# mLSTM row sums as a 257th value column of the numerator products

## What is computed

```python
sc = jnp.einsum('bhtd,bhsd->bhts', qc, kc) * jnp.exp(D - m_t[..., None])
num = jnp.einsum('bhts,bhsd->bhtd', sc, vc) + inter[..., None] * (...)
den = sc.sum(-1) + inter * (...)
h = num / jnp.maximum(jnp.abs(den), jnp.exp(-m_t))[..., None]
```

## Time and profile before

| | us |
|---|---|
| median of 3 runs | 1370.7 |
| lowest, highest | 1369.31, 1373.73 |
| profiled execution | 1371.72 |
| its span | 1369.7 |
| mean granted clock of TensorE | 0.988 |
| TensorE, VectorE, ScalarE, GpSimd busy | 1343.4, 800.8, 639.0, 206.5 |

### The profile page before, as it was taken

One profiled execution on the slowest core, in us unless ns is written; L12 is line 12 of the kernel. 1 busy time (PEld: TensorE's weight loads), 2 busy tenths in 40 slices (PEclk: granted clock), 3 DMA queues, 4 the chain that ended last, 5 costly groups with the idle time before them and its releaser, 6 DMA issues.

```text
span 1369.7 us, 16279 instructions
## 1 busy us (share of the span) xinstructions
PE 1343.4 (98%) x6400; PEld 1108.8 (81%) x6400; DVE 800.8 (58%) x1180; ACT 639.0 (47%) x883; POOL 206.5 (15%) x248
## 2 busy tenths in 40 slices
PE   9999999999999999999799999999999999999995
PEld 8888888888788888888688888888888888888884
DVE  5655555555657664865764554555546576657656
ACT  5445445444455543443444454454444555435432
POOL 0410310311211000300311122121121200003002
PEclk9999999999999999999999999999999999999998
DMA  9864664664466566466376646646635656555562
GB/s 314 268 182 132 187 175 138 184 172 136 138 181 187 170 200 202 148 189 199 107 239 187 175 129 190 179 129 190 178 108 166 187 174 191 173 200 166 185 192 87
DMA packets 127002, 240.86 MB, mean 176 GB/s; under 512 B 12048, under 2 KB 12080, under 8 KB 126416
## 3 DMA queue, kind: packets, MB, share of 16 engines
q1 hardware_dynamic: 123936, 230.85, 56.1%
q0 software_dynamic: 1632, 6.90, 1.4%
q10 hardware_dynamic: 1360, 2.10, 0.4%
HBM read 237.72 MB, written 2.10 MB: 175 GB/s over the span
## 4 chain that ended last, share of the span: by engine, by line
PE 90%; DVE 5%; ACT 2%; DMA 2%; issue 0%; SPq 0%; DVEq 0%; ACTq 0%
PE ps L302 81%; DMA w_raw<-w_in_dram 2%; DVE w_lo L812 1%; ACT w_hi L600 1%; PE ps L403 1%; DVE xres L1133 1%; PE ps L377 1%; PE ps L535 1%; ACT arena L651 1%; DVE xres L1122 1%; PE ps L319 1%; PE ps L414 1%; PE ps L416 1%; PE ps L418 1%; PE ps L392 1%; PE ps L390 1%
## 5 line engine op out<-in xcount | busy, mean ns | idle before, releaser
L812 DVE TENSOR_TENSOR w_lo<-w_raw,w_hi 128x1024 fp32r<-128x1024 f32 x432 | 559.1, 1299 | 507.7 <-ACT w_hi L600 507.6
L600 ACT ACTIVATE w_hi<-w_raw 128x1024 fp32r<-128x1024 f32 x432 | 455.0, 1057 | 569.5 <-PE ps L302 538.2
L302 PE MATMUL ps<-w_hi,xT_hi 128*128 128x512 f32 x1724 | 686.5, 398 | 1.1 <-DVE w_lo L812 0.6
L302 PE MATMUL ps<-w_hi,xT_lo 128*128 128x512 f32 x1724 | 674.9, 392 | 0.0
L302 PE MATMUL ps<-w_lo,xT_hi 128*128 128x512 f32 x1724 | 673.3, 391 | 0.0
L302 PEld LDWEIGHTS ps<-w_hi,xT_hi 128*128 128x128 f32 x1724 | 325.3, 189 | 70.8 <-issue 4.7
L302 PEld LDWEIGHTS ps<-w_hi,xT_lo 128*128 128x128 f32 x1724 | 324.9, 188 | 69.9
L302 PEld LDWEIGHTS ps<-w_lo,xT_hi 128*128 128x128 f32 x1724 | 325.7, 189 | 64.8
L651 ACT ACTIVATE arena<-arena,nmax 128x128 f32<-128x128 f32 x96 | 42.5, 444 | 39.2 <-DVE nmax L895 39.2
L233 POOL TENSOR_TENSOR carried<-sel 1x1 f32<-1x1 f32 x16 | 8.9, 559 | 225.4 <-DVE arena L1028 178.7
L1210 POOL TENSOR_TENSOR su<-z,sincos 128x128 f32<-128x128 f32 x24 | 10.6, 461 | 211.9 <-DVE z L829 211.9
(11 more groups left out here) (218 smaller groups left out, 845.8 us busy)
## 6 DMA issues: line engine op xcount, KB each, us to landing
w_raw<-w_in_dram SPq DMA_DIRECT2D x368, 512.0 KB, 3.7
w_raw<-w_out_dram SPq DMA_DIRECT2D x64, 512.0 KB, 4.5
mix<-x_t_dram SPq DMA_DIRECT2D x8, 256.0 KB, 6.0
xres<-x_dram ACTq DMA_DIRECT2D x4, 512.0 KB, 11.5
arena<-ln_g_dram POOLq DMA_DIRECT2D x2, 1024.0 KB, 6.0
arena<-ln_b_dram POOLq DMA_DIRECT2D x2, 1024.0 KB, 8.2
out_dram<-xres SPq DMA_DIRECT2D x8, 256.0 KB, 2.7
hg<-head_g_dram POOLq DMA_DIRECT2D x4, 256.0 KB, 7.6
```

The costliest lines, as they stand in the source:

```text
L302: mm = pe.matmul(ps[2 * s + t][:], a[:, order[c] * KC + k, t * P:(t + 1) * P], b[:, c % RING, k], start=(c + k + i == 0), stop=(c == CH - ...
L600: A(w_hi[:, c % RING], w_raw[:, c % RING], ACT.Copy).then_inc(w_hi_done, 1)
L812: TTn(w_lo[:, c % RING], w_raw[:, c % RING], w_hi[:, c % RING].bitcast(F32), ALU.subtract).then_inc(w_lo_done, 1)
```

## The change

- `vM` becomes [token tile, head, 257]: the 257th column of each head is 1.0, set by a memset on VectorE in each layer (`V.memset(vM[:, :, :, MD:MD + 1], 1.0)`). `scE` moves by eight columns to make room. The copies of v (`take`) write two runs of 256 with a column left out between them.
- The twelve row-sum matmuls per layer are gone. Each numerator matmul has 257 columns, and its last output column is the row sum.
- A head's two outputs lie in two banks: token tiles 0 and 1 of head h in banks 6 and 7 for an even h, 4 and 5 for an odd one.
- VectorE computes the reciprocal per head, in front of the product: two tensor_tensor (maximum with exp(-m)), two scalar_tensor_tensor (times -1, maximum), a reciprocal, with a wait after each kind.
- The first transposes of `mix` wait for all four `h_done`, as `mden_done` is gone and bank 4 and 5 hold numerators.

```diff
--- before.py
+++ after.py
@@ -102,8 +102,8 @@
         og = arena[:, 5376:6400].rearrange("p (t c) -> p t c", t=TT)
         oacc = arena[:, 6400:7424].rearrange("p (t c) -> p t c", t=TT)
         qkT = arena[:, 0:4096].rearrange("p (m t) -> p m t", m=KT)
-        vM = arena[:, 4096:6144].rearrange("p (t c) -> p t c", t=TT)
-        scE = arena[:, 6144:7680].rearrange("p (h s) -> p h s", h=MH)
+        vM = arena[:, 4096:4096 + TT * MH * (MD + 1)].rearrange("p (t h c) -> p t h c", t=TT, h=MH)
+        scE = arena[:, 6152:7688].rearrange("p (h s) -> p h s", h=MH)
         lngb = arena[:, 0:4096].rearrange("p (a c) -> p a c", a=2)
         conv_y = sb("conv_y", [P, 2, 2, SEQ])
         decay = sb("decay", [P, MH, 3 * P])
@@ -163,7 +163,7 @@
         gcum, ga, gmax, gm = (conv_y[0:MH, i // 2, i % 2, :] for i in range(4))
         gem = sb("gem", [MH, SEQ])
         gcol = sb("gcol", [P, 2, TT, MH])
-        den = sb("den", [P, 3, TT, MH])
+        den = sb("den", [P, 2, TT, MH])
         stats = sb("stats", [P, TT, 4, 6])
         mv = sb("mv", [P, TT, 4, 2])
         rstd = sb("rstd", [P, 2, TT, 4])
@@ -203,7 +203,7 @@
             sem("conv_ps"), sem("conv_bias"), sem("conv_done"), sem("conv_silu"))
         ag_silu, mg_silu, mo_sigmoid = sem("ag_silu"), sem("mg_silu"), sem("mo_sigmoid")
         msc_ps, msc_done = sem("msc_ps"), sem("msc_done")
-        mden_ps, mden_done, mnum_ps, h_done = sem("mden_ps"), sem("mden_done"), sem("mnum_ps"), sem("h_done")
+        mnum_ps, den_done, h_done = sem("mnum_ps"), sem("den_done"), sem("h_done")
         h_root, h_norm = sem("h_root"), sem("h_norm")
         mix_att, mix_ml = sem("mix_att"), sem("mix_ml")
         ln_stats, ln_root, ln_rstd, ln_norm = sem("ln_stats"), sem("ln_root"), sem("ln_rstd"), sem("ln_norm")
@@ -541,14 +541,7 @@
                     mlstm_scores(h)
                 chunks(N_MV + 1, Q_MV + 1, 1, MH, CH)
                 chunks(N_MG1, Q_MG1, 0, 0, 1)
-
                 pe.wait_ge(msc_done, (l + 1) * MH)
-                for h in range(MH):
-                    pe.matmul(ps[4][:, h:h + 1], scE[:, h, 0:P], ones[:], start=True, stop=True)
-                    pe.matmul(ps[4][:, MH + h:MH + h + 1], scE[:, h, P:2 * P], ones[:], start=True, stop=False)
-                    mm = pe.matmul(ps[4][:, MH + h:MH + h + 1], scE[:, h, 2 * P:3 * P], ones[:],
-                                   start=False, stop=True)
-                mm.then_inc(mden_ps, 1)
                 for h in range(MH):
                     chunks(N_MG1, Q_MG1, 0, 1 + h, 2 + h)
                     if h == 0:
@@ -557,17 +550,17 @@
                         pe.wait_ge(sgu_done, l + 1)
                     if h >= 2:
                         pe.wait_ge(h_done, l * MH + h - 1)
-                    o, v = ps[6 + h % 2], slice(h * MD, (h + 1) * MD)
-                    pe.matmul(o[:, 0:MD], scE[:, h, 0:P], vM[:, 0, v], start=True, stop=True)
-                    pe.matmul(o[:, MD:2 * MD], scE[:, h, P:2 * P], vM[:, 0, v], start=True, stop=False)
-                    mm = pe.matmul(o[:, MD:2 * MD], scE[:, h, 2 * P:3 * P], vM[:, 1, v],
+                    o = 6 - 2 * (h % 2)
+                    pe.matmul(ps[o][:, 0:MD + 1], scE[:, h, 0:P], vM[:, 0, h, :], start=True, stop=True)
+                    pe.matmul(ps[o + 1][:, 0:MD + 1], scE[:, h, P:2 * P], vM[:, 0, h, :], start=True, stop=False)
+                    mm = pe.matmul(ps[o + 1][:, 0:MD + 1], scE[:, h, 2 * P:3 * P], vM[:, 1, h, :],
                                    start=False, stop=True)
                     mm.then_inc(mnum_ps, 1)
                 chunks(N_MG1, Q_MG1, 0, 5, CH)
 
 
                 chunks(N_SG, Q_SG, 1, 0, 4)
-                transposes(mix, CH, OUT_ORDER, 0, ((mden_done, l + 1), (mix_att, l + 1)))
+                transposes(mix, CH, OUT_ORDER, 0, ((h_done, (l + 1) * MH), (mix_att, l + 1)))
                 transposes(mix, CH, OUT_ORDER, 1)
                 chunks(N_SG, Q_SG, 1, 4, CH)
                 first_block(N_OUT, Q_OUT, mix, CH, OUT_ORDER, 2, {
@@ -700,7 +693,10 @@
 
                 def take(n, s, dst):
                     act.wait_ge(w_used, used(l, n, -1))
-                    A(dst, ps[2 * s][:], ACT.Copy).then_inc(z_act, 1)
+                    src = ps[2 * s][:]
+                    if len(dst.shape) == 3:
+                        src = src.rearrange("p (h d) -> p h d", d=MD)
+                    A(dst, src, ACT.Copy).then_inc(z_act, 1)
 
                 take(N_SU, 0, mix[:, 0, 2 * BW:3 * BW])
                 act.wait_ge(gates_ps, l + 1)
@@ -752,10 +748,10 @@
                 n = N_MV + 1
                 split(n, 0, 4)
                 act.wait_ge(mix_att, l + 1)
-                take(n, 0, vM[:, 0, 0:BW])
+                take(n, 0, vM[:, 0, 0:2, 0:MD])
                 split(n, 4, 8)
                 split(N_MG1, 0, 4)
-                take(N_MG1, 1, vM[:, 0, BW:2 * BW])
+                take(N_MG1, 1, vM[:, 0, 2:4, 0:MD])
                 A(store[:, 1:3], store[:, 1:3], ACT.Sigmoid).then_inc(mo_sigmoid, 1)
                 split(N_MG1, 4, 8)
                 split(N_SG, 0, 2)
@@ -826,7 +822,10 @@
                 def take(n, s, dst):
 
                     dve.wait_ge(w_used, used(l, n, -1))
-                    V.tensor_copy(dst, ps[2 * s + 1][:]).then_inc(z_dve, 1)
+                    src = ps[2 * s + 1][:]
+                    if len(dst.shape) == 3:
+                        src = src.rearrange("p (h d) -> p h d", d=MD)
+                    V.tensor_copy(dst, src).then_inc(z_dve, 1)
 
                 if l == 0:
                     for c in range(CH):
@@ -1020,7 +1019,8 @@
                 n = N_MV + 1
                 split(n, 0, 4)
                 dve.wait_ge(mix_att, l + 1)
-                take(n, 0, vM[:, 1, 0:BW])
+                V.memset(vM[:, :, :, MD:MD + 1], 1.0)
+                take(n, 0, vM[:, 1, 0:2, 0:MD])
                 dve.wait_ge(decay_done, l + 1)
                 for h in range(MH):
                     split(n, 4 + h, 5 + h)
@@ -1033,8 +1033,18 @@
                     dve.wait_ge(mnum_ps, l * MH + h + 1)
                     def at(t):
                         return store[:, 1 + h // 2, t, (h % 2) * MD:(h % 2 + 1) * MD]
+                    o = 6 - 2 * (h % 2)
                     for t in range(TT):
-                        f = STT(at(t), ps[6 + h % 2][:, t * MD:(t + 1) * MD], den[:, 1, t, h:h + 1], at(t),
+                        f = TTn(den[:, 0, t, h:h + 1], ps[o + t][:, MD:MD + 1], gcol[:, 1, t, h:h + 1], ALU.max)
+                    own(f)
+                    for t in range(TT):
+                        f = STT(den[:, 0, t, h:h + 1], ps[o + t][:, MD:MD + 1], -1.0, den[:, 0, t, h:h + 1],
+                                ALU.mult, ALU.max)
+                    own(f)
+                    V.reciprocal(den[:, 1, :, h], den[:, 0, :, h]).then_inc(den_done, 1)
+                    dve.wait_ge(den_done, l * MH + h + 1)
+                    for t in range(TT):
+                        f = STT(at(t), ps[o + t][:, 0:MD], den[:, 1, t, h:h + 1], at(t),
                                 ALU.mult, ALU.mult)
                     own(f)
                     for t in range(TT):
@@ -1046,17 +1056,9 @@
                     f.then_inc(h_done, 1)
 
                 split(N_MG1, 0, 4)
-                take(N_MG1, 1, vM[:, 1, BW:2 * BW])
+                take(N_MG1, 1, vM[:, 1, 2:4, 0:MD])
                 split(N_MG1, 4, 5)
 
-                dve.wait_ge(mden_ps, l + 1)
-                sums = ps[4][:, 0:TT * MH].rearrange("p (t h) -> p t h", t=TT)
-                own(TS(den[:, 0], sums, -1.0, None, ALU.mult))
-                own(TTn(den[:, 0], sums, den[:, 0], ALU.max))
-                own(TTn(den[:, 2], den[:, 0], gcol[:, 1], ALU.max))
-                f = V.reciprocal(den[:, 1], den[:, 2])
-                f.then_inc(mden_done, 1)
-                dve.wait_ge(mden_done, l + 1)
                 dve.wait_ge(mo_sigmoid, l + 1)
                 for h in range(3):
                     split(N_MG1, 5 + h, 6 + h)
```

## The result

| | before | changed |
|---|---|---|
| median, us (4 runs each) | 1371.2 | 1360.79 |
| lowest, highest | 1369.31, 1373.73 | 1358.9, 1362.33 |
| profiled execution, its span | 1371.72, 1369.7 | 1358.90, 1357.2 |
| mean granted clock in it | 0.988 | 0.992 |

More runs of the same two kernels came with the experiments. There the kernel before took 1371.6 us on average (34 runs) and the changed one 1363.4 (12 runs): 8.2 us. With the four first runs the changed one comes to 1362.7 (16 runs, 1358.9 to 1367.1): **8.9 us**. The four runs first compared, mean 1360.7, were thus low for the changed kernel; whether by luck or by something about that first comparison is not shown. Both 8.2 and 8.9 are still more than the forecast.

The account below looks back on a forecast made before the run. The prediction took TensorE, busy for 98% of the span, to bound the kernel. Its terms gave 1371.7 - 5.4 - 1.6 + 0.04 = 1364.7 us, settled at 1364.5, with a range from 1361.8 to 1368.0.

Parts of the forecast that it names:

- What bounds the kernel: Whole kernel: TensorE, busy 98% of the span; time removed there counts, work added on VectorE is free within its lead.
- The row sums, 5.4 us: TensorE, both layers: removing the 24 one-column matmuls saves 2 x 2.7 = 5.4 us.
- The clock behind them, 1.6 us: TensorE, layer 2, behind the row sums: the half-clock stretch goes with them, saving 1.6 us.
- 1365.3 if in none, 1363.7 if in one, 1362.1 if in both: Forecast time in us, by how many layers of the median run had the clock drop behind the row sums.
- The range: Whole kernel: 1361.8 us, just below two clock drops saved, to 1368.0, with half the three runs' 4.4 us spread.
- 257 columns, 0.04 us: TensorE, 24 numerator instructions: one more column each, 0.0017 us a column, adds 0.04 us in all.
- Rival 3: Numerators on TensorE: odd width halves the rate, costing 10.3 us, 1375.0; chance 0.04 slower, 0.04 with a smaller price.
- VectorE, 0.85 us per head: VectorE, each head: five small instructions and three waits take 0.85 us, covered by 0.81 us of idle time.
- The near bound: VectorE's new work per head: 0.73 us, from pairs as short as bn_aggr's 0.22; the far bound is 1.50.
- The lead ahead of numerator 2: Head 0 done before numerator 2 starts on TensorE: 3.5 us, less 0.85 and 0.3, leaves 2.3 us.
- Rival 2: VectorE's per-head work becomes the pace and TensorE waits at numerators 2 and 3: 1368.7 us; chance 0.09.
- Rival 1: TensorE's clock drop is not tied to the row sums, or returns elsewhere in layer 2: 1366.3 us; chance 0.18.

Follow-up runs that it names:

- the block: The changed kernel with the twelve one-column row-sum matmuls per layer put back together at their old place, result unread: median 1371.15 us, ratio to the kernel before 1.0002.
- the spread row sums: The changed kernel with the same one-column matmuls, three ahead of each head's numerator: median 1370.87 us, ratio to the kernel before 0.9989.
- the split gates: The changed kernel with two of the four small gate matmuls moved ahead of the last projection chunk of their block: 1364.04 us, beside 1363.70 for the changed kernel.

## Why the prediction was wrong, point by point

Two steps failed. The term "1.6 us" for the clock behind the row sums was too small, 2.5 ± 0.5 measured. And the low end of the range put at nothing what the rest of the execution does differently from run to run: 5.5 us between the two profiled executions.

- **What bounds the kernel**: right. Whatever left TensorE's stream came off the end, and what was added on VectorE within its lead did not come on.
- **The row sums, 5.4 us**: right. 2.73 us per layer in the timeline, 5.9 ± 0.3 from all runs without the clock.
- **The clock behind them, 1.6 us**: the mechanism is right, the size is the term that was too small. I took one stretch per execution, since the one trace had one. On average the block costs 2.5 ± 0.5 us; at 1.6 us each, an estimate from this is that about three of four blocks are followed by a half-clock stretch. The two traces with blocks have it behind one of two each, both times in layer 2. My own step "1365.3 if in none, 1363.7 if in one, 1362.1 if in both" named the cases; the trace of one execution could not say how often each comes. With 2.5 for 1.6 the sum reads 1371.6 - 5.4 - 2.5 + 0.1 = 1363.8, against a mean of 1362.7 ± 0.6. What is left, 1.1 us, is within two standard errors of the two means (0.7) and has no place that I could name; with the clock taken out the kernels differ by 6.1 ± 0.4. The sum also starts from a trace with three half-clock stretches inside its layers, and the prediction counts two: the one behind the gate matmuls of layer 2 is missing from it.
- **The range**: its low end, "just below two drops saved", left no room for what varies anyway. Single runs of the changed kernel lie between 1358.9 and 1367.1. Half-clock stretches behind the gate matmuls come or not (0 to 2 of 1.6 us each), and the start takes 65.3 to 67.3 us to the first head transposes in eight traces, and 69.4 and 70.6 in those of the spread row sums and the split gates, where TensorE waited 2.2 and 2.4 us for a w_lo at 43 to 44 us and a half-clock stretch followed. I gave the upper end such room and the lower none. The four runs first compared (mean 1360.7) lost 11.5 ± 0.7 us to the clock, 3.8 less than the kernel before where 1.6 were forecast, and lie 6.9 us under it without the clock where 5.4 were: that put them outside. The profiled one of them has no half-clock stretch behind the gate matmuls and the fastest start of all ten traces, neither of which comes from the change.
- **257 columns, 0.04 us**: 0.06 to 0.07 per layer, 0.13 in all, with the banks and VectorE in it. Nothing. Rival 3, the odd width, did not occur: 0.218 us a record for 0.215. The Trainium skill ("SBUF — State Buffer", the note on SBUF cachelines) has a penalty for each crossing to a new line; no more than these 3 ns can be seen of it.
- **VectorE, 0.85 us per head**: 0.71. The near bound, built on the bn_aggr pair, was 0.73 and would have been the better choice. The lead ahead of numerator 2 was put at 2.3 us and is 2.6. Rival 2 did not occur; 0.7 us more per head is free, 2.7 us more costs 7 us per layer (14.5 in all).
- **Rival 1**, the clock not tied to the row sums: refuted by the block against the spread. The Trainium skill ("TensorE: Matmul & The Clock Gate", section "Why this matters for your kernels") speaks of idle gaps; this case shows that, and more. At the layer border, where TensorE waits 5.4 and 1.9 us, the clock is at 0.50 for 10.2 us (678.4 to 688.6 in the kernel before). But in the window of the block TensorE is busy 3.00 of 3.00 us, and the clock falls to 0.50 behind it all the same.

## What to carry over

A matmul of a single column costs 0.22 us here, half of what 256 columns take (0.43), and the loads of its weights fill that time. If the same weights are used again soon, another column of that later matmul is all but free: 0.07 us per layer, for twelve instructions saved that took 2.7. When TensorE sets the time and its clock varies, read more than one execution before you size a clock term, and give the range room for it on both sides; the mean clock of the runs parts it from the rest. Small matmuls spread between large ones lost less to the clock than in a block, both times; but the time gained was 1.0 ± 0.6 us for the row sums and none for the gate matmuls, where each further place cost a switch of 0.5 us.

## What was not expected of the hardware

- The granted clock fell to 0.50 for 3.4 us behind blocks of small matmuls in which TensorE had no idle time, in some executions and not in others. The two blocks of 24 one-column records (2.6 us each) cost 2.5 ± 0.5 us of clock per execution on top of their own 5.4; spread by threes the same matmuls cost none that can be seen.
- Switching from float32 to float32r matmuls costs nothing behind a numerator: the first projection matmul stands 0.43 us ahead of the next instead of 0.23 (535.14 to 535.57 in the changed kernel), but the numerator before it stands only 0.24 ahead of it instead of 0.43 (534.90), so both take the usual 0.67. Behind one-column matmuls it costs 0.10. Cutting the block of small gate matmuls in two costs 0.5 us per layer.
- Two independent 128x1 instructions on VectorE take 0.22 us together, when one of eight columns takes 0.17.
